# Gate, branch and output projections of the last stage: each weight panel as seven half-size products of quarter sums instead of eight

## The reference, cut to what matters

```python
g_na, g_pool, g_rw = jnp.split(jax.nn.sigmoid(keep(merge_logits)), N_BRANCH, axis=-1)   # merge_logits: part of h @ w_in
merged = g_na * (b_na @ w_branch[0]) + g_pool * (b_pool @ w_branch[1]) + g_rw * (b_rw @ w_branch[2])
out = merged @ w_out
...
return x_lat + gate_l[:, None] * out, None      # then rms_norm(x_lat, final_g)
```

## Time and profile before

| | |
|---|---|
| median of 3 runs | 4093.5 us (4091.15 to 4094.21) |
| profiled execution, its own time | 4089.74 us |
| its span, first to last instruction | 4087.9 us |
| TensorE busy | 3912.8 us, 96% of the span |
| VectorE busy | 1101.2 us, 27% |
| ScalarE busy | 654.3 us, 16% |
| mean granted TensorE clock | 0.974 |

### The profile page before, as it was taken

One profiled execution on the slowest core, in us unless ns is written; L12 is line 12 of the kernel. 1 busy time (PEld: TensorE's weight loads), 2 busy tenths in 40 slices (PEclk: granted clock), 3 DMA queues, 4 the chain that ended last, 5 costly groups with the idle time before them and its releaser, 6 DMA issues.

```text
span 4087.9 us, 60574 instructions
## 1 busy us (share of the span) xinstructions
PE 3912.8 (96%) x27010; PEld 2659.8 (65%) x27010; DVE 1101.2 (27%) x2366; ACT 654.3 (16%) x1509; POOL 184.1 (5%) x263
## 2 busy tenths in 40 slices
PE   5999999899999999999999999999999988999998
PEld 3446745454444666787667686666666667888887
DVE  1000143751012332213002520444554453000001
ACT  2100022420001122212001300222222221000000
POOL 0000000000000000000000000221111121000000
PEclk9999999999999999999999999999999987999999
DMA  8443323224433433464443133110111100444443
GB/s 342 176 154 124 124 93 114 83 83 166 154 133 105 184 124 114 149 233 147 152 154 124 62 135 131 57 34 33 44 44 44 34 23 23 154 155 155 154 155 124
DMA packets 73491, 489.68 MB, mean 120 GB/s; under 512 B 8448, under 2 KB 10496, under 8 KB 19472
## 3 DMA queue, kind: packets, MB, share of 16 engines
q1 hardware_dynamic: 70560, 462.45, 32.0%
q0 software_dynamic: 2672, 23.35, 1.5%
HBM read 481.57 MB, written 4.19 MB: 119 GB/s over the span
## 4 chain that ended last, share of the span: by engine, by line
PE 92%; DVE 3%; DMA 2%; ACT 1%; POOL 1%; issue 1%; DVEq 0%; ACTq 0%; POOLq 0%
PE ps L953 51%; PE ps L1053 9%; PE ps L947 7%; PE ps L1218 4%; PE ps L892 3%; PE ps L1013 3%; PE ps L1032 2%; PE ps L1203 2%; PE ps L950 2%; PE ps L1023 1%; POOL zone L830 1%; PE ps L1122 1%; PE ps L1289 1%; DMA lamv<-in_lam 1%; PE ps L900 1%
## 5 line engine op out<-in xcount | busy, mean ns | idle before, releaser
L953 PE MATMUL ps<-h,w 128*128 128x256 f32 (+1 forms) x4992 | 1546.6, 461 | 24.1 <-ACT h L1538 14.2
L953 PEld LDWEIGHTS ps<-h,w 128*128 128x128 f32 x4992 | 935.7, 192 | 475.8 <-issue 380.3
L953 PE MATMUL ps<-y,w 128*128 128x256 f32 (+1 forms) x1792 | 505.3, 441 | 0.0
L953 PEld LDWEIGHTS ps<-y,w 128*128 128x128 f32 x1792 | 338.9, 190 | 152.7 <-issue 119.9
L1053 PE MATMUL ps<-h,w 128*128 128x256 f32 (+1 forms) x1024 | 413.3, 521 | 1.3 <-issue 1.3
L947 PE MATMUL ps<-w,h 128*128 128x256 f32 x1280 | 280.4, 380 | 0.0
L947 PEld LDWEIGHTS ps<-w,h 128*128 128x128 f32 x1280 | 242.4, 190 | 39.4 <-issue 7.3
L1053 PEld LDWEIGHTS ps<-h,w 128*128 128x128 f32 x1024 | 176.7, 194 | 91.8 <-issue 69.3
L1854 DVE TENSOR_TENSOR modc<-ps,bmod 128x4 f32<-128x4 f32 x72 | 11.3, 157 | 709.1 <-PE ps L900 709.1
L1218 PEld LDWEIGHTS ps<-zone 64*64 64x64 f32 x4608 | 153.9, 139 | 47.9 <-issue 33.0
L1218 PE MATMUL ps<-zone 64*64 64x64 f32 x4608 | 175.1, 226 | 1.5 <-DVE zone L2139 1.4
(11 more groups left out here) (306 smaller groups left out, 3043.6 us busy)
## 6 DMA issues: line engine op xcount, KB each, us to landing
w<-in_wm SPq DMA_DIRECT2D x144, 1024.0 KB, 7.7
w<-in_we SPq DMA_DIRECT2D x52, 1024.0 KB, 5.0
w<-in_w SPq DMA_DIRECT2D x48, 1024.0 KB, 5.1
w<-in_wmg SPq DMA_DIRECT2D x48, 1024.0 KB, 5.1
w<-in_wi SPq DMA_DIRECT2D x34, 1024.0 KB, 5.1
w<-in_wo SPq DMA_DIRECT2D x32, 1024.0 KB, 5.0
w<-in_wrw SPq DMA_DIRECT2D x32, 1024.0 KB, 5.1
w<-in_wbr SPq DMA_DIRECT2D x48, 512.0 KB, 4.2
```

The source lines that it names most:

```text
L953: last = mm(pass_psum(s, q), rows[:, n * P:(n + 1) * P], src[k], start=(k == 0), stop=(k == s.kt - 1))
```

## The change

Every panel of the last stage is cut in quarters: input tiles in a first and a second half (hk = kt / 2), output channels in two times 128. The 256 tokens are cut in two times 128, so that the activations have quarters b11 (first half of the input tiles, first 128 tokens), b12, b21, b22. `product(F, n)` does seven products of hk matmuls each, every one a 128 x 128 weight tile against 128 tokens, into four PSUM banks a panel. They read the weights' quarters and four sums s1 to s4 of them (s3 is written beside, a21 stays as it is), and the activations' quarters and four sums t1 to t4.

DVE forms the weights' sums of every panel (`sums`, three of them in `sum_bufs`; four instructions over hk x 128 elements), and those of the activations once for each source (`tee`): of `h` during `rw_recur(7)`, of the three branches' y at the start and in j = 0 and 1, of `merged` in j = 23 and behind it. GpSimd forms the sums of the first panel. The results are put together from PSUM by one ACT copy (`keep_first`), two DVE additions (`common`), three more (`fourth`, `third`, `second`) and one ACT instruction (`first_quarter`); gates take a further tanh over the three other quarters (`other_quarters`). `merge` combines gate and branch over a whole panel (512 elements), once instead of twice. The first product of the first panel is moved ahead of `rw_variance(7)`.

The panels now have three places of 16 KB a partition (the two buffers of `w` and the tile `xc`, here `xcf`), and SP fetches a panel in two halves at once when the last product of the place's former panel is through. The core of the diff:

```diff
...
+        m1 = z(11776, 2, P)
+        u2, u3 = z(16832, 2, P), z(17088, 2, P)
...
+        def quarters(x, hk):
+            return x[:, 0:hk, 0:P], x[:, 0:hk, P:NL], x[:, hk:2 * hk, 0:P], x[:, hk:2 * hk, P:NL]
...
+        h_parts = quarters(h[:, :, NC:T], 8)
+        h_sums = h[:, 0:8, 0:P], h[:, 0:8, P:NC], h[:, 8:16, P:NC], h[:, 8:16, 0:P]
...
+        fast_slots = [w[:, rw_first % 2, :], xcf, w[:, 1 - rw_first % 2, :]]
+        sum_bufs = [z(12224, 3, 8, P), z(5632, 3, 8, P), z(8704, 3, 4, P)]
...
+        def add_fast(kind, j, src, slot, sums, b, t, banks, kt):
+            hk = kt // 2
...
+        for j in range(24):
+            i, b = j // 3, j % 3
+            add_fast("mg", j, A["wmg"][8 * b + i, :, :], j % 2, j % 2, h_parts, h_sums, (0, 1, 3, 6), KT)
+            add_fast("br", j, A["wbr"][8 * b + i, :, :], 2, 2, y_parts[b], y_sums[b], (2, 4, 5, 7), 8)
+        for j in range(8):
+            add_fast("out", j, A["wout"][j, :, :], j % 3, j % 2, m_parts, m_sums, (0, 1, 3, 6), KT)
+        fetch_order = [0, 1, 2]
+        for j in range(23):
+            fetch_order += [2 * j + 4 if j < 22 else 48, 2 * j + 3]
+        fetch_order += range(49, 56)
...
+            for f in fetch_order:
+                F = fasts[f]
+                if F.after is not None:
+                    sp.wait_ge(s_prod, 7 * F.after + 7)
+                elif F.slot == 1:
+                    sp.wait_ge(s_fold, 8)
+                    sp.wait_ge(s_rr, 16)
+                else:
+                    sp.wait_ge(s_rwp, 30 if F.slot == 0 else 32)
+                n = F.hk * COLS
+                for half in range(2):
+                    sp.dma_start(fast_slots[F.slot][:, half * n:half * n + n], F.src[:, half * n:half * n + n])\
+                        .then_inc(s_gw[F.slot], 16)
...
+            F = fasts[0]
+            pool.wait_ge(s_gw[F.slot], 32)
+            tt(F.s[0], F.a[2], F.a[3], ALU.add).then_inc(s_pool, 1)
+            pool.wait_ge(s_pool, 1)
+            tt(F.s[1], F.s[0], F.a[0], ALU.subtract).then_inc(s_pool, 1)
+            tt(F.s[2], F.a[0], F.a[2], ALU.subtract)
+            pool.wait_ge(s_pool, 2)
+            tt(F.s[3], F.a[1], F.s[1], ALU.subtract).then_inc(s_sum0, 1)
...
+            def product(F, n):
+                f = F.f
+                same = f - 1 if F.kind == "out" else f - 2
+                (a11, a12, _, a22), (s1, s2, s3, s4), (b11, _, b21, b22), (t1, t2, t3, t4) = F.a, F.s, F.b, F.t
+                left, right, bank = ((a11, b11, 0), (s2, t2, 1), (s3, t3, 2), (s1, t1, 3), (a12, b21, 0), (a22, t4, 2),
+                                     (s4, b22, 3))[n]
+                if n == 0:
+                    pe.wait_ge(s_gw[F.slot], 32 * F.use)
+                    if same >= 0:
+                        pe.wait_ge(s_c11, same + 1)
+                    if f == 5:
+                        pe.wait_ge(s_ct, 8)
+                    if f == 48:
+                        pe.wait_ge(s_md, 12)
+                elif n == 1:
+                    if f == 0:
+                        pe.wait_ge(s_sum0, 1)
+                        pe.wait_ge(s_th, 1)
+                    else:
+                        pe.wait_ge(s_sum, f)
+                    if F.kind == "br" and F.j < 3:
+                        pe.wait_ge(s_ty, F.j + 1)
+                    if f == 48:
+                        pe.wait_ge(s_tm, 1)
+                elif n == 2:
+                    if same >= 0:
+                        pe.wait_ge(s_c12, same + 1)
+                elif n == 4:
+                    pe.wait_ge(s_m1, f + 1)
+                elif n == 5:
+                    pe.wait_ge(s_u3, f + 1)
+                elif n == 6:
+                    pe.wait_ge(s_c22, f + 1)
+                for k in range(F.hk):
+                    last = mm(ps[:, F.banks[bank], 0:P], left[:, k, :], right[:, k, :], start=(n < 4 and k == 0),
+                              stop=(k == F.hk - 1), skip_group_check=True)
+                last.then_inc(s_prod, 1)
...
             rw_mean(7)
+            pe.wait_ge(s_rwe, 32)
+            product(fasts[0], 0)
             rw_variance(7)
-            pe.wait_ge(s_rwe, 32)
+            for n in range(1, 7):
+                product(fasts[0], n)
             pe.wait_ge(s_yc, 16)
-            for j in range(24):
-                run(project("mg", [j]))
-                run(project("br", [j]))
-            run(project("wout"))
+            for F in fasts[1:]:
+                for n in range(7):
+                    product(F, n)
...
+            def keep_first(F):
+                act.wait_ge(s_prod, 7 * F.f + 1)
+                if F.f >= 2:
+                    act.wait_ge(s_u3, F.f - 1)
+                f(m1[:, F.f % 2, :], ps[:, F.banks[0], 0:P], ACT.Copy).then_inc(s_m1, 1)
+            def first_quarter(F):
+                act.wait_ge(s_prod, 7 * F.f + 5)
...
+                o, src = result(F)[:, 0:P], ps[:, F.banks[0], 0:P]
+                if F.kind == "mg":
+                    f(o, src, ACT.Tanh, scale=0.5).then_inc(s_c11, 1)
+                else:
+                    f(o, src, ACT.Copy).then_inc(s_c11, 1)
+            def other_quarters(F):
+                act.wait_ge(s_c12, F.f + 1)
+                v = result(F)[:, P:4 * P]
+                f(v, v, ACT.Tanh, scale=0.5).then_inc(s_tanh, 1)
+            def squares(j):
+                for t in (2 * j, 2 * j + 1):
+                    act.wait_ge(s_xr, t + 1)
...
+                    f(lacc3 if t == 0 else lsq3[:, t % 2, :], xl[:, t, :], ACT.Square).then_inc(s_lsq, 1)
...
             rw_square(7)
+            keep_first(fasts[0])
             rw_root(7)
             for j in range(24):
...
-            layer_root(6, 0, NL)
+                if j >= 1:
+                    keep_first(fasts[2 * j])
+                first_quarter(fasts[2 * j])
+                other_quarters(fasts[2 * j])
+                keep_first(fasts[2 * j + 1])
+                first_quarter(fasts[2 * j + 1])
+            for j in range(8):
+                keep_first(fasts[48 + j])
+                if j >= 1:
+                    squares(j - 1)
+                first_quarter(fasts[48 + j])
+            squares(7)
...
+            def tee(b, t, rows=slice(None), done=None):
+                b11, b12, b21, b22 = (v[:, rows, :] for v in b)
+                t1, t2, t3, t4 = (v[:, rows, :] for v in t)
+                link(v_.tensor_tensor(t1, b12, b11, ALU.subtract))
+                yield
+                link(v_.tensor_tensor(t2, b22, t1, ALU.subtract))
+                yield
+                v_.tensor_tensor(t3, b22, b12, ALU.subtract)
+                yield
+                last = v_.tensor_tensor(t4, b21, t2, ALU.subtract)
+                if done is not None:
+                    last.then_inc(done, 1)
+                yield
+            def tee_spread():
+                dve.wait_ge(s_rwp, 32)
+                yield
+                for _ in tee(h_parts, h_sums, done=s_th):
+                    yield
+                    yield
             def rw_recur(it):
-                beside = rw_features(it + 1) if it < 7 else iter(())
+                beside = rw_features(it + 1) if it < 7 else tee_spread()
...
+            def sums(F):
+                a11, a12, a21, a22 = F.a
+                s1, s2, s3, s4 = F.s
+                dve.wait_ge(s_gw[F.slot], 32 * F.use)
+                if F.f >= 3:
+                    dve.wait_ge(s_prod, 7 * (F.f - (3 if F.f == 49 else 4 if F.kind == "mg" or F.f == 48 else 2)) + 7)
+                link(v_.tensor_tensor(s1, a21, a22, ALU.add))
+                yield
+                link(v_.tensor_tensor(s2, s1, a11, ALU.subtract))
+                yield
+                v_.tensor_tensor(s3, a11, a21, ALU.subtract)
+                yield
+                v_.tensor_tensor(s4, a12, s2, ALU.subtract).then_inc(s_sum, 1)
+                yield
+            def part(F, n):
+                return ps[:, F.banks[n], 0:P]
+            def common(F):
+                dve.wait_ge(s_prod, 7 * F.f + 2)
+                dve.wait_ge(s_m1, F.f + 1)
+                if F.f >= 2:
+                    dve.wait_ge(s_c12, F.f - 1)
+                link(v_.tensor_tensor(u2[:, F.f % 2, :], part(F, 1), m1[:, F.f % 2, :], ALU.add))
+                dve.wait_ge(s_prod, 7 * F.f + 3)
+                v_.tensor_tensor(u3[:, F.f % 2, :], part(F, 2), u2[:, F.f % 2, :], ALU.add).then_inc(s_u3, 1)
+            def fourth(F):
+                dve.wait_ge(s_prod, 7 * F.f + 4)
+                dve.wait_ge(s_u3, F.f + 1)
...
+                v_.tensor_tensor(result(F)[:, 3 * P:4 * P], part(F, 3), u3[:, F.f % 2, :], ALU.add).then_inc(s_c22, 1)
+            def third(F):
+                dve.wait_ge(s_prod, 7 * F.f + 6)
+                v_.tensor_tensor(result(F)[:, 2 * P:3 * P], part(F, 2), u2[:, F.f % 2, :], ALU.add)
+            def second(F):
+                dve.wait_ge(s_prod, 7 * F.f + 7)
+                v_.tensor_tensor(result(F)[:, P:2 * P], part(F, 3), u2[:, F.f % 2, :], ALU.add).then_inc(s_c12, 1)
```

(139 more changed lines are left out.)

48 lines of the change are left out of this document (19 added, 29 removed).

## The result

| | before | after |
|---|---|---|
| median of 4 runs each | 4092.3 us (4083.5 to 4094.2) | 4046.9 us (4041.6 to 4051.4) |
| profiled execution, its own time | 4089.7 us | 4045.5 us |
| ratio to the kernel before, 95% interval | | 0.989 (0.9876 to 0.9904) |

What follows compares the result with a forecast made beforehand. The last stage was taken as bound by TensorE's weight-load and matmul pairs, at 0.1115 us each. Savings 45.8 + 10.6, less 1.1, 1.7, 1.9 and 0.8, gave 50.9, so 4042.5 us; 8-in-10 range 4028 to 4063.

Steps and rivals of the forecast that it cites:

- Rival B: Last stage: weight loads do not keep 0.1115 us a pair over hundreds of pairs; 4235 at 0.151; chance 0.09.
- the estimate of 4160: Last stage: 25 ns more a matmul in a sustained stream, so 4928 pairs at 0.1365 take 673 us; about 4160.
- Rival C: Last stage: a pair takes 0.107 to 0.109 us; with 0.107, 22 us more saved, 4020; chance 0.09.
- Steps 1 and 5: 23 gate-and-branch pairs: 18.73 us instead of 20.72, 45.8 saved; `tee` in j = 1 and 23 loses 1.7.
- Steps 2 and 6: Eight output panels: 12.49 us instead of 13.81, 10.6 saved; transition from last branch panel to output loses 1.9.
- The steady ledger: Steady gate-and-branch pairs: DVE and ACT work timed against TensorE's waits; no stall, least slack 1.4 us.
- Rival A: Gate-and-branch pairs: DVE or a transfer is late in every pair; 4066 with 1 us, 4090 with 2; chance 0.17.
- Rival D: Last stage: DVE's sums become the pace at 20.7 us a pair, no gain, about 4093; chance 0.03.
- Step 4, start of the stage: First gate and branch panels: waits on DVE and ACT end the branch panel near 3486.4 instead of 3485.3; 1.1 lost.
- Step 4, "GpSimd's four sums cost nothing": First panel's sums: some 8 us on GpSimd, whose queue is idle for 46.6 us; 0 lost.
- Step 7, tail: Behind the last matmul: `second` and two additions instead of one addition of 0.48 us; 0.8 lost.

Runs made afterwards that it cites:

- e5_delay3: The changed kernel with three more DVE additions of 1.22 us in every pair of panels, between the branch panel's sums and `fourth`: 4104.72 us, ratio 1.0037.
- e1_pool_alone: The kernel before, with only GpSimd's four sums of 1024 elements added behind the last fold, their results unused: 4092.95 us, ratio 1.0008.
- e2_sums_on_dve: The changed kernel with the first panel's four sums moved from GpSimd to DVE, between the state updates of `rw_recur(7)`: 4036.89 us, ratio 0.9871.
- e7_late_fetch: e3_gaps with the fetch of the third panel's 2 MB held back until the second state update of `rw_recur(7)`: 4031.8 us, ratio 0.9858.
- e3_gaps: e2_sums_on_dve with the first branch's `tee` in the short gaps of `rw_recur(7)` and six rows of `merged` split over j = 22 and 23: 4037.09 us.
- e3_again: e3_gaps run once more unchanged, beside e7_late_fetch on one chip: 4035.65 us, ratio 0.9865.
- e4_delay1: The changed kernel with one more DVE addition of 1.22 us in every pair of panels, between the branch panel's sums and `fourth`: 4048.77 us, ratio 0.9903.
- e6_eight: The changed kernel with product 0 of every panel computed twice, so eight products instead of seven: 4118.68 us, ratio 1.0068.

## Why the prediction was right, and where it was off

- **The new matmuls.** Right. A burst of eight gave 0.1115 us a pair, and 3696 pairs without a gap take 0.1116. Rival B is refuted, and with it the estimate of 4160 from the Trainium skill (TensorE: Matmul & The Clock Gate, section Back-to-back issue gap); that section's further 25 ns don't exist here for float32 pairs (0.1116 sustained, 0.1115 in the burst). Rival C (0.107) is refuted as well.
- **Steps 1 and 5** (pairs of panels and `tee`): 44.0 against 44.1, in part by luck. A pair took 18.76 us instead of 18.73, 0.7 more over 23, and the `tee` cost 0.8 in j = 23 and nothing in j = 1, where 1.7 was worked out. **Steps 2 and 6** (output panels and transition): 8.5 against 8.7, and the stall 1.95 against 1.9.
- **The steady ledger.** Right on what it was for: no stall. e5_delay3 tested its number for `fourth` and found it within 0.2 us. The margin that it named, 1.4 us, was not the one that counts: it is that of the branch panel's u3, whose `common` waits for a product and not for DVE. What DVE can lose is the 1.9 us of `fourth`. Rival A is refuted for the change as it is; e5_delay3 shows that it was the true danger, since 3.7 us of DVE work more a pair make the kernel slower than before. Rival D too.
- **Step 4, start of the stage.** The stretch was 2.1 us shorter than forecast, from two errors of about 1 us. The gate panel ended 20.05 us behind mean(7) instead of 21.0. Its stalls were forecast as 1.5 + 1.3 at u3 and c22 and came as one of 2.8. The half clock was taken to last until `rw_readout(7)` as in the earlier trace rows, and it ended behind product 0 (3470.27, 4.4 us into the stage instead of 9), probably because product 0 fills TensorE where it idled; no run tried it. The 16 half-clock pairs behind the stall took 1.5 of this back. The branch panel took 6.57 us instead of 7.7: of the 1.5 us that the `tee` of the second branch was to cost it, 0.2 came.
- **Step 4, "GpSimd's four sums cost nothing".** This step failed, and with it 5.8 us. It asked only who waits for the sums. It did not ask what runs on DVE beside them, and their size was taken from the earlier trace rows at 512 elements, so that some 8 us in all became 9.8. e1_pool_alone has the loss without the change, and e2_sums_on_dve has the change without these stretched instructions. The rows divide the 5.8: 4.5 of longer wait and 1.3 of lower clock behind it, and nothing for the `tee` of `h`, as forecast. That taking the sums off GpSimd gives only 2.8 back has another cause: the issue stall (2.0 of the 3.0 that stay), which comes out when the wait is gone; in the change the same transfer (issued at 3421.48) lies under the wait of 5.89.
- **The fetch of the third panel** was costed only by when it lands. Its issue stall of 0.9 to 2.0 us was not in any rival.
- **Step 7, tail:** 1.1 against 0.8.

Together: 53.5 saved in the stage, 1.1, 5.8 and 2.4 lost outside, 44.2. The forecast of 4042.5 was 4.4 us low. In the profiled pair 6.7 us are missing against the 50.9: the collision (5.8) and the scatter ahead of it (2.4), less the 2.1 at the start of the stage. So the mechanism in the stage was right, and the sum lay in its range because the term that was left out is small beside it.

## What to carry to other kernels

Work that is moved to an idle engine needs two questions: who waits for its result, and what else uses the same ports while it runs; here some 10 us of GpSimd work beside three short DVE instructions made a wait of TensorE 5.9 us long instead of 1.4, and the clock cost 1.3 us more behind it. A chain of small dependent instructions (the inversion) is a bad neighbour for bulk GpSimd work and, it seems, for a 2 MB transfer; the dense stage behind it bears such transfers, and no run tried GpSimd there. Where a stage is bound by the count of one instruction, a short burst of exactly that shape in the old trace priced 3696 of them to 0.1%.

## What the runs showed of the hardware

- A GpSimd addition of float32 with both inputs in SBUF takes 2.36 to 2.53 us at 1024 elements, and stretches a DVE instruction of 0.48 with two SBUF inputs to 0.3 us behind its own end (2.44). One with a PSUM input keeps its 0.64.
- TensorE can stand still for 0.9 to 2.0 us, marked as issue, while a 2 MB transfer of weights is under way, in a stretch of short matmuls (64 x 64, 0.029 us a pair); with the transfer moved 15 us later, in e7_late_fetch, it did not. In the dense stage at 0.112 a pair, with a DMA share of 0.47, it never did.
- The same idle time of 1.95 us at the same place left the granted clock at 1.00 in the profiled execution of the change (3928.9 to 3931.0) and took it to 0.58 in that of e2_sums_on_dve (3918.3 to 3922.0). In the five other profiled executions with this idle time (e3_gaps, e3_again, e7_late_fetch, e4_delay1, e5_delay3) the product behind it took the 2.02 us that it took in the change. What decides is open.
- Behind an idle time of 5.7 to 5.9 us in the last inversion the clock was at its lower level in all five profiled executions that have it (the change, e1_pool_alone, e4_delay1, e5_delay3, e6_eight), for instance at 0.55 over 3.3 us in the change and at 0.50 over 6 us in e1_pool_alone; behind 1.36 us, in the kernel before, it was at 1.00.
